# A seven-product FFN: VectorE's queue laid out anew, and one weight sum moved from a DMA to VectorE

## What is computed

```python
def swiglu(x, w_gate, w_up, w_down):
    return (jax.nn.silu(x @ w_gate) * (x @ w_up)) @ w_down

hdn = rmsnorm(x, gains[0])
x = x + 0.5 * rmsnorm(swiglu(hdn, w_gate, w_up, w_down), gains[1])   # D_MODEL = 1024, D_FF = 2816
```

## Time and profile before

| | |
|---|---|
| median of 3 runs | 2628.32 us (2625.51 to 2629.8) |
| the profiled execution | 2626.27 us |
| its span, first to last instruction | 2623.2 us |
| TensorE busy / VectorE busy / ScalarE busy | 95% / 60% / 41% of the span |
| mean granted TensorE clock | 0.984 of 2.4 GHz |
| products of the four FFNs (L773) | from 74.9 us to 2467 us, 6048 matmuls |

### The profile page before, as it was taken

One profiled execution on the slowest core, in us unless ns is written; L12 is line 12 of the kernel. 1 busy time (PEld: TensorE's weight loads), 2 busy tenths in 40 slices (PEclk: granted clock), 3 DMA queues, 4 the chain that ended last, 5 costly groups with the idle time before them and its releaser, 6 DMA issues. The chain is left out here.

```text
span 2623.2 us, 50681 instructions
## 1 busy us (share of the span) xinstructions
PE 2488.5 (95%) x19669; PEld 2350.9 (90%) x19669; DVE 1574.4 (60%) x2730; ACT 1069.4 (41%) x2026; POOL 537.5 (20%) x745
## 2 busy tenths in 40 slices
PE   8899999998999989999989999999989989899998
PEld 7899999995557989999989999999979969899998
DVE  6877426546664677752587762467545665787623
ACT  4544324224443444442445442334354434454422
POOL 0111003023331211100211100255255532011001
PEclk9999999999999999999999999999999999899999
DMA  4577422348994257752147763223210143477531
GB/s 127 140 169 173 120 79 69 78 137 299 309 306 135 61 121 169 172 133 85 57 107 167 172 151 89 54 73 88 62 33 1 33 112 90 105 169 170 141 89 46
DMA packets 456589, 320.79 MB, mean 122 GB/s; under 512 B 14440, under 2 KB 410933, under 8 KB 456360
## 3 DMA queue, kind: packets, MB, share of 16 engines
q1 hardware_dynamic: 424112, 241.90, 32.5%
q0 software_dynamic: 32272, 76.04, 13.5%
HBM read 270.58 MB, written 9.56 MB: 107 GB/s over the span
## 5 line engine op out<-in xcount | busy, mean ns | idle before, releaser
L773 PE MATMUL ps<-x_part_hi,part_hi 128*128 128x272 f32 x2016 | 592.4, 294 | 48.4 <-DVE part_lo L823 20.1
L773 PE MATMUL ps<-x_part_hi,part_lo 128*128 128x272 f32 x2016 | 587.8, 292 | 0.0
L773 PE MATMUL ps<-x_part_lo,part_hi 128*128 128x272 f32 x2016 | 584.9, 290 | 0.0
L508 DVE TENSOR_TENSOR w_lo<-w_raw,w_hi 128x1024 fp32r<-128x1024 f32 (+1 forms) x170 | 245.3, 1443 | 505.4 <-ACT w_hi L501 500.8
L501 ACT CAST w_hi<-w_raw 128x1024 fp32r<-128x1024 f32 (+1 forms) x170 | 199.0, 1170 | 618.1 <-PE ps L536 560.7
L773 PEld LDWEIGHTS ps<-x_part_hi,part_hi 128*128 128x128 f32 x2016 | 383.9, 190 | 56.1 <-DVE part_lo L823 24.7
L773 PEld LDWEIGHTS ps<-x_part_lo,part_hi 128*128 128x128 f32 x2016 | 384.8, 191 | 0.0
L773 PEld LDWEIGHTS ps<-x_part_hi,part_lo 128*128 128x128 f32 x2016 | 383.9, 190 | 0.0
L536 PE MATMUL ps<-hd_hi,w_hi 128*128 128x272 f32 x1408 | 294.3, 290 | 4.4 <-DVE w_lo L508 4.3
L536 PE MATMUL ps<-hd_lo,w_hi 128*128 128x272 f32 x1408 | 291.6, 289 | 0.0
L536 PE MATMUL ps<-hd_hi,w_lo 128*128 128x272 f32 x1408 | 291.3, 288 | 0.0
(11 more groups left out here) (567 smaller groups left out, 4655.5 us busy)
## 6 DMA issues: line engine op xcount, KB each, us to landing
w_raw<-in_ffn_w_down_dram SPq DMA_DIRECT2D x64, 704.0 KB, 4.5
w_pair<-in_ffn_w_gate_dram SPq DMA_DIRECT2D x72, 512.0 KB, 5.3
w_pair<-in_ffn_w_up_dram SPq DMA_DIRECT2D x72, 512.0 KB, 5.4
v_pages<-in_cache_a_v_dram POOLq DMA_DIRECT2D x128, 256.0 KB, 4.5
w_sums<-w_pair POOLq DMA_DIRECT2D x72, 256.0 KB, 3.3
w_pair<-w_pair POOLq DMA_DIRECT2D x72, 256.0 KB, 4.6
w_raw<-in_c_w_in_dram SPq DMA_DIRECT2D x33, 512.0 KB, 4.0
k_pages<-in_cache_a_k_dram SPq DMA_DIRECT2D x64, 256.0 KB, 4.3
```

Of the source, the lines that this page charges most:

```text
L508: e.tensor_tensor(w_lo[:, n % 2, 0:nk * P], raw[:, n % RAW, 0:nk * P], w_hi[:, n % 2, 0:nk * P].bitcast(F32), ALU.subtract).then_inc(sem(" ...
L773: mm = e.matmul(ps[:, bank, 0:TH], w[:, k * P:(k + 1) * P], x[:, k, :], start=idx < 4 and k == 0 and w is wh and x is xp_hi[idx], stop=k = ...
```

## The change

It does five things. (1) t3 = b12 + b22 is no longer loaded and summed by DMAs but added by VectorE (`dve_t3`), just ahead of t2; the third load goes, the first accumulating DMA goes, and the second, b12 += b11, is issued by GpSimd when t3 is done. Part 2 of a pair waits for that DMA; t2 and part 3 wait for VectorE alone. (2) In the plain stage VectorE's order changes: xn goes ahead of split 4 and of gate 1, x_sums ahead of split 6, the first three x_parts ahead of split 7. (3) low 0 and low 1 are put off until just ahead of part 0, low 2 and low 3 until steps 14 and 15. (4) Plain tile 3 (gate, up, silu, hidden, high) is taken out of the run-up and done at steps 3 to 6; x_part 5 goes ahead of step 0 and x_part 6 to step 1 (ScalarE: step 0). (5) `hidden` writes to a tile of its own (`h_early`), tile 3 and the first pair's u_sum and w_sum get free memory in `h_raw`, and waits for `low` become waits for `hidden`.

```diff
         def vector_steps():
-            steps = [("gate", 0), ("up", 0), *(("xn", x) for x in range(KD)), ("hidden", 0), ("low", 0), ("gate", 1), ("up", 1)]
-            steps += [*(("xn", x) for x in range(KD, 2 * KD)), ("hidden", 1), ("low", 1), *(("x_sum", n) for n in range(4))]
-            steps += [("gate", 2), ("up", 2), *(("x_part", n) for n in range(3)), ("hidden", 2), ("low", 2)]
-            steps += [("part", 0), ("t2", 0), ("part", 1), ("gate", 3), ("part", 2), ("x_part", 3), ("part", 3), ("t4", 0)]
-            steps += [("x_part", 4), ("part", 4)]
+            steps = [("gate", 0), ("up", 0), *(("xn", x) for x in range(KD)), ("hidden", 0), *(("xn", x) for x in range(KD, 2 * KD))]
+            steps += [("gate", 1), ("up", 1), *(("x_sum", n) for n in range(4)), ("hidden", 1), *(("x_part", n) for n in range(3))]
+            steps += [("gate", 2), ("up", 2), ("hidden", 2), ("low", 0), ("low", 1), ("part", 0), ("t3", 0), ("t2", 0), ("part", 1)]
+            steps += [("part", 2), ("x_part", 3), ("part", 3), ("t4", 0), ("x_part", 4), ("part", 4), ("x_part", 5)]
...
-                e.dma_start(part_rows(w_sums[x][:, 0, :]), of[p % 2][:, 0:KH, m2]).then_inc(sem(f"w_pair{p % 2}"), 16)
...
             for p in range(WP):
                 x = home(g, p)
                 pair_landed(e, f, p)
-                b11, b21, b12, b22 = (w_pair[x][:, c, k:k + KH, :] for c in range(2) for k in (0, KH))
-                t3, t2 = (part_rows(w_sums[x][:, y, :]) for y in range(2))
-                e.dma_start(t3, b22, accum_op=ALU.add).then_inc(sem(f"w_added{p % 2}"), 16)
-                e.dma_start(b12, b11, accum_op=ALU.add).then_inc(sem(f"w_added{p % 2}"), 16)
+                wait_step(e, "vector", f, "t3", p)
+                e.dma_start(w_pair[x][:, 1, 0:KH, :], w_pair[x][:, 0, 0:KH, :],
+                            accum_op=ALU.add).then_inc(sem(f"w_added{p % 2}"), 16)
...
         def act_part(e, g, q):
...
-            if idx == 1:
-                wait_step(e, "vector", f, "t2", p)
-            if idx in (2, 3):
-                added(e, f, p, 2)
-            if idx == 6:
-                wait_step(e, "vector", f, "t4", p)
+            if idx in (1, 3, 6):
+                wait_step(e, "vector", f, {1: "t2", 3: "t3", 6: "t4"}[idx], p)
+            if idx == 2:
+                added(e, f, p, 1)
...
+        def dve_t3(e, g, p):
+            f, x = ffn_of(g), home(g, p)
+            pair_landed(e, f, p)
+            e.tensor_tensor(part_rows(w_sums[x][:, 0, :]), w_pair[x][:, 1, 0:KH, :], w_pair[x][:, 1, KH:KD, :],
+                            ALU.add).then_inc(sem("ffn_vector"), did("vector", "t3", p))
+
         def dve_t2(e, g, p):
             f, x = ffn_of(g), home(g, p)
-            added(e, f, p, 2)
+            wait_step(e, "vector", f, "t3", p)
...
             xn(2, 1, 0, 0, plus)
             xn(0, 0, 0, KH, plus)
+            dve_split(e, first + 4, 0, KD)
             hidden(0)
-            low(0)
-            dve_split(e, first + 5, 0, KD)
+            xn(6, 1, KH, 2 * KH, minus)
+            xn(4, 0, KH, 3 * KH, plus)
             gate(1)
             up(1)
...
                 if q + RING < PROD * WP:
                     dve_part(e, g, q + RING)
                     if (q + RING) % PROD == 0:
+                        dve_t3(e, g, (q + RING) // PROD)
                         dve_t2(e, g, (q + RING) // PROD)
                     if (q + RING) % PROD == 3:
                         dve_t4(e, g, (q + RING) // PROD)
-                if q < 2:
-                    dve_x_part(e, g, 5 + q)
-                if q == 0:
+                if q == 1:
+                    dve_x_part(e, g, 6)
+                if q == 3:
+                    gate(3)
                     up(3)
-                if q == 2:
+                if q == 5:
                     hidden(3)
-                if q == 4:
-                    low(3)
+                if q in (2 * PROD, 2 * PROD + 1):
+                    low(2 + q - 2 * PROD)
```

More of the change, by code:

```diff
@@ L624, in vector_steps @@
                 steps += [("pair_low", prev)] * (idx == 2 and p % 2 == 0 and p > 0 and prev < LATE // 2)
[L625 to L628, removed]
+                if q + RING < PROD * WP:
+                    steps += [("part", q + RING)]
+                    steps += [(x, (q + RING) // PROD) for x in {0: ("t3", "t2"), 3: ("t4",)}.get((q + RING) % PROD, ())]
+                steps += [("x_part", 6)] * (q == 1)
+                steps += {3: [("gate", 3), ("up", 3)], 5: [("hidden", 3)], 2 * PROD: [("low", 2)], 2 * PROD + 1: [("low", 3)]}.get(q, [])
                 steps += [("late", x) for x in late_at(q) if q < PROD * WP - 1]
-            return [x for x in steps if x[0] not in DMA_SUMS] + [("gated", KU - 1)] + [("late", x) for x in range(7, KF - LATE)]
+            return steps + [("gated", KU - 1)] + [("late", x) for x in range(7, KF - LATE)]
         def scalar_steps():
-            steps = [("silu", 0), ("high", 0), ("silu", 1), ("x_part", 0), ("high", 1), ("x_part", 1), ("x_part", 2), ("silu", 2)]
-            steps += [("high", 2), ("part", 0), ("part", 1), ("silu", 3), ("part", 2), ("x_part", 3), ("part", 3), ("x_part", 4)]
-            steps += [("part", 4)]
+            steps = [("silu", 0), ("x_part", 0), ("high", 0), ("silu", 1), ("x_part", 1), ("x_part", 2), ("high", 1), ("silu", 2)]
+            steps += [("high", 2), ("part", 0), ("part", 1), ("part", 2), ("x_part", 3), ("part", 3), ("x_part", 4)]
+            steps += [("part", 4), ("x_part", 5)]
             for q in range(PROD * WP):
@@ L928, in act_gate_up @@
                     if p == 1:
-                        wait_step(e, "vector", f, "low", 2 * STD - 1)
+                        wait_step(e, "vector", f, "hidden", 2 * STD - 2)
                     elif prev < LATE // 2:
@@ L961, in dve_sums @@
             to = up_buf if p % 2 else gate_buf
+            u_sum, w_sum = ((rb if p else h_raw[:, 2 * STD, :])[:, half_of(x)] for x in range(2))
             if idx == 1:
                 wait_step(e, "scalar", f, "p1", p)
-                wait_step(e, "vector", f, *(("sums", p - 1) if p else ("up", 2 * STD - 1)))
+                if p:
+                    wait_step(e, "vector", f, *(("sums", p - 1) if p > 1 else ("up", 2 * STD - 1)))
                 e.tensor_tensor(u_sum, ps[:, bank + 1, 0:TH], p1_out[:, :],
@@ L974, in dve_sums @@
                 if p < 2:
-                    wait_step(e, "vector", f, ("hidden", "low")[p], 2 * STD - 1)
+                    wait_step(e, "vector", f, "hidden", 2 * STD - 2)
                 else:
@@ L998, in up @@
                 if j >= 2:
[L999 to L1000 removed]
+                    wait_step(e, "vector", f, "hidden", j - 2)
+                e.tensor_tensor(halves(plain_up(j)), cols(4 * (j % 2) + 2), halves(rb[:, :]),
                                 ALU.mult).then_inc(sem("ffn_vector"), did("vector", "up", j))
@@ L1028, in dve_gate_up @@
             up(0)
-            dve_split(e, first + 4, 0, KD)
             xn(2, 1, 0, 0, plus)
             xn(0, 0, 0, KH, plus)
+            dve_split(e, first + 4, 0, KD)
             hidden(0)
-            low(0)
-            dve_split(e, first + 5, 0, KD)
+            xn(6, 1, KH, 2 * KH, minus)
+            xn(4, 0, KH, 3 * KH, plus)
             gate(1)
             up(1)
[L1037 to L1041, removed]
+            dve_split(e, first + 5, 0, KD)
             for n, (to, a, b, op) in enumerate(X_SUMS):
@@ L1045, in dve_gate_up @@
                                 op).then_inc(sem("ffn_vector"), did("vector", "x_sum", n))
+            hidden(1)
+            dve_split(e, first + 6, 0, KD)
+            for n in range(3):
+                dve_x_part(e, g, n)
             dve_split(e, first + 7, 0, KD)
@@ L1048, in dve_gate_up @@
             up(2)
-            for n in range(3):
-                dve_x_part(e, g, n)
             hidden(2)
-            low(2)
+            low(0)
+            low(1)
             dve_part(e, g, 0)
+            dve_t3(e, g, 0)
             dve_t2(e, g, 0)
             dve_part(e, g, 1)
-            gate(3)
             dve_part(e, g, 2)
```

43 lines of the change are left out of this document (23 added, 20 removed).

## The result

The change makes the kernel slower: 2802.26 us (median of 4 runs, 2796.51 to 2807.28) against 2626.91 us (4 runs, 2624.6 to 2629.8), a ratio of 1.0671, 95% interval 1.0653 to 1.0689. Forecast were 2720 us, in a range of 2645 to 2785. The sign and the stage were right; the loss, 175 us, is nearly twice the 92 forecast and lies outside the range.

What follows compares the result with a forecast made beforehand. TensorE, busy 95% of the span, was taken as the bound, so only its idle time and slow stretches could be won. Profiled 2626.27 us - 30 (starts) + 122 (pairs) = 2718, as median 2720; range 2645 to 2785.

Steps and rivals of the forecast that it cites:

- The starts: Start of each FFN's product stage, last plain matmul to product 9: the new order gains 30 us in all.
- The loop: Product stage: VectorE from part 2 to next t3, GpSimd's DMA, ScalarE's cast, next part 2; +122 us in four FFNs.
- d: Time of the accumulating DMA from issue to landing, in each pair: taken as 4.0 us, ends 3.3 and 4.7.
- GpSimd's hand-over: In each pair, the time for GpSimd to see t3 before it issues the DMA: 0.10 us, an estimate.
- the rival of the loads (c): Product stage: loads ahead of the accumulating DMA hold it up, d = 5.5 us; 2816 us, chance 0.07.
- (a): Product stage: the loop does not bind and VectorE's short order pays, d below 2.3 to 2.5; 2596 us, chance 0.11.
- The faster transfer (b): Product stage: the lone accumulating DMA is faster than any before, d = 2.6, gain and loss cancel; 2630 us, chance 0.07.
- The clock (d): Product stage: idle time in each pair lowers TensorE's clock, 0.8 us in each of 64 pairs; 2770 us, chance 0.05.
- Small parts: Plain tile 3 done late among the products, and the other buffers of the plain tiles: cost nothing.

Runs made afterwards that it cites:

- run 1: The changed kernel with weight sums as before (three loads, two accumulating DMAs a pair, no t3 on VectorE), new order kept: 2602.16 us, ratio 0.9905.
- run 2: The kernel before with only t3 moved to VectorE, two loads and one accumulating DMA for each pair: 2816.2 us, one execution.
- run 6: The changed kernel without the sum b12 + b11: GpSimd issues nothing, part 2 takes b12 as loaded, t3 stays on VectorE: 2594.39 us, one execution.
- run 7: The changed kernel with b12 += b11 done by an addition on GpSimd, not by its DMA: 2602.64 us, ratio 0.9906.
- Run 4: The changed kernel with the loads of pair p waiting until the accumulating DMA of pair p-1 has landed: 2722.04 us, one execution.
- run 5: The changed kernel with the edits of run 3 and Run 4 together: 2600.38 us, ratio 0.9907.
- run 3: The changed kernel with t3 of pair p at step 0 of pair p-1 instead of step 2: 2656.55 us, ratio 1.0109.
- run 8: The changed kernel with both t3 and b12 += b11 done by additions on GpSimd: 2616.53 us, ratio 0.9959.

## Why the prediction was right and wrong

**The starts (right).** -30.7 us measured, -30 forecast; each start within 1.5 us of its own forecast (19.09, 18.70, 18.84, 18.15 against 17.8, 19.1, 18.7, 19.6). That the sum is closer still is luck: +1.3 in the first FFN and -1.4 in the fourth cancel. By run 1 the order gives 22.9 of it, so the rest needed t3 on VectorE. The gap ahead of product 5 for w_sum is there in all four, 2.5 us at the longest, the gap at product 1 is gone. In the second FFN product 5 starts 10.7 us after the plain units, 3.1 us late where 4.4 were forecast; behind it a short stretch at the lower clock (0.91 in that window) takes some of the difference away again.

**The loop as mechanism (right).** ScalarE's cast of part 2 waits for the DMA in 71 places. Runs 1 and 2 place the loss in t3's move, 6 shows that the same work on VectorE costs next to nothing without the wait (pairs at 731.1 us for 725.2), 7 that the same dependences cost little (733.7) when the sum takes 1.9 us. VectorE's piece of the loop was forecast as 6.66 us from the earlier trace rows and measured as 6.57, the way from the landing to part 2 as 0.77 and measured as 0.74.

**Its length (wrong): the term d, and GpSimd's hand-over.** The pairs cost +203.9 us against +122: 82 us short. The 64 turns from t3 to t3 (pairs 1 to 16 in each of four FFNs) show where: together they take 895 us, 81 more than the forecast's 4 x (139.5 + 64) = 814. In them d, from issue to landing, is 4.82 us on the mean (4.71 over all 72 transfers), where I took 4.0: 0.82 x 64 = 52 us. From t3's end to GpSimd's issue lie 0.55 us on the mean, not 0.10: 0.45 x 64 = 29 us. That is the whole of it. The other pieces come out as forecast: VectorE's work, t3 included, 504.5 us against 502.2, and the way from the landing to part 2 47.7 against 49.3. For an odd pair 12.1 was forecast and 13.27 measured, and d's 0.70 and the hand-over's 0.44 are the difference.

Both errors could have been bounded from what was shown. I had argued that the new transfer is "alone but inside the loads' traffic", and then priced it between the best and the worst of transfers issued ahead of the loads; the slower family, went to a rival. Run 4 shows what its traffic costs: 1.5 us in most pairs. So the rival of the loads (c) was the right reason, and d's excess over 4.0 came to half of what it said. Its time, 2816 us, is near the measured 2802 by luck, since it left out the hand-over too. My upper end of 4.7 for d stood just below where the mean came to lie. The hand-over got one value, an estimate, and no upper bound at all, although it is paid 64 times. With 4.82 and 0.55 in their places the forecast's own sum gives 2799 us.

**The rivals.** That the loop doesn't bind (a) is refuted by run 2; its 2596 us is what runs 5 to 7 give once the loop is shortened, 2594 to 2603. The faster transfer (b) is refuted: none of the 72 took under 3.2 us. With it goes the estimate of 2.6 us by the Trainium skill, "DMA: Bandwidth & Descriptors", section "Anatomy of one DMA", which has no accumulation in it. The clock (d) is small: stretches at the lower level in each FFN, means of 0.97 to 0.99, which the loop, holding no product, mostly hides. No run isolates it, but the turns bound it: a slower TensorE could lengthen them only through VectorE's waits for products, and VectorE's piece of all 64 turns, waits included, is 2 us above the forecast where the rival had 51.

**Small parts.** Priced at nothing, and run 6 agrees, within 6 us: the pairs at 731.1 against 725.2 before, t3 and the late tile 3 included. What they cost is in pairs 2 and 4, at 12.5 and 12.7 us each in run 6.

## What to carry to other kernels

Ahead of moving one addition from a DMA to an in-order engine, write down the ring that it closes: which engine must finish what before the DMA may start, and which instruction of the same engine then waits for its landing. A ring costs nothing as long as it is shorter than the work of the engine that sets the pace, and its whole excess in every turn beyond that; so each hand-over in it needs its own upper bound, and fixes that fall short one by one (runs 3 and 4) may pass together (run 5). The new order of the starts is worth having, 1% with any of runs 1, 5 and 7; which of the three is best, 2600.4, 2602.2 or 2602.6, their intervals don't tell.

## What the runs showed of the hardware

- A DMA issued by GpSimd on VectorE's release starts 0.54 or 0.55 us after VectorE's instruction ends in 62 of 72 places, and 0.56 to 0.64 in the others; a computing instruction of GpSimd, in the same place, 0.14 us after (run 7).
- An accumulating transfer of 256 KB within SBUF takes 3.2 to 3.3 us alone (the medians of runs 4 and 5), and a median of 4.8 to 4.9 us with the next pair's loads issued beside it. How far apart they are issued counts. In the changed kernel the median is 4.8 us where the first of the two loads stands 2.1 us ahead (44 transfers), 3.5 where it stands 3.3 us ahead (11). In run 3 it is 4.9 us where that load stands 0.4 us behind. In run 4, 8 of 72 take 4.4 to 5.4 us with no load beside them; the cause is open.
- GpSimd's addition of 128x512 float32 takes 1.73 us where VectorE's takes 0.69, and while it runs VectorE's low part of the same size may take 1.61 us (run 8). One such addition in a pair left the pairs within 3 us of the kernel without the sum (run 7 against run 6), two cost 14 us more.
